# Two layer norms applied behind the projection: the query projection and the first pair of the up projection read the un-normed sum

## The chip, the cores and the metric

The kernel runs on one core of one Trainium2 chip. The metric is the device time of one execution in microseconds (us). A difference of 0.2% (1.8 us) is about what a measurement of this kernel can tell from no change.

## The reference, cut to what matters

Two transformer blocks run one after the other on 256 tokens of width 1024, in fp32. The change lies in the first block, between its token mixer and its feed-forward layer:

```python
def layer_norm(x, g, b):
    mu = xf.mean(-1, keepdims=True)
    var = jnp.square(xf - mu).mean(-1, keepdims=True)
    return (xf - mu) * lax.rsqrt(var + EPS) * g + b

h = hybrid_mixer(x, w_in, ...)                    # ends with ... @ w_out
x = layer_norm(ALPHA * x + h, ln1_g, ln1_b)
h = memory_cross_attention(x, mem, wq, wkv, wo)   # q = x @ wq; softmax attention over 256 memory rows; @ wo
x = layer_norm(ALPHA * x + h, ln2_g, ln2_b)
h = conv_ffn(x, w_up, conv_w, conv_b, w_down)     # u = conv(x @ w_up); (gelu(g) * val) @ w_down
x = layer_norm(ALPHA * x + h, ln3_g, ln3_b)
```

With s the sum before the norm, W a weight matrix and r the reciprocal deviation, `layer_norm(s) @ W = r * ((s * g) @ W - mu * (g @ W)) + b @ W`. The mean and the deviation belong to a token, so they can be applied after the product.

## The kernel before, in words

Activations are kept transposed: `X` holds the residual stream as 8 tiles of 128 features by 256 tokens. A matrix product in fp32 accuracy is made of three products of fp32r operands: each operand is split in a high part (an ACT copy, line 142) and a low part (a DVE subtraction, line 145); `three` (L415) multiplies high by high, low weights by high input, high weights by low input. For the input these parts are `INH` and `INL` (or `HIH` and `HIL`), for the weights `hir` and `lor`.

A **unit** is one product with 256 output features over 8 input tiles (`linears_g`, L435): 48 matmuls of 256 columns, six for each input tile k. Its weights come as two tiles of 4 k each, 512 KB from memory into one of six slots of `raw`; `stage` (L337) splits a tile into one of four buffers of `hir` and `lor`: one ACT copy of 128x1024 and one DVE subtraction of 128x1024. `take` (L381) stages up to three tiles ahead, where a buffer's last reader has already been issued. A tile of the modulation weights of the second block costs one DVE pass instead (`mod_step`, L331, shown as a write to `raw,small`). `linears` of two keys is a **pair**: the two units advance together over k.

Every engine works through its own queue strictly in the order in which this program appends instructions, so an ACT copy of a weight tile that stands behind another ACT instruction waits for it, and the DVE subtraction waits for the ACT copy. All waits are semaphores that the code sets.

The place of the change, in the order of the program:

- Output projection `wout` (L1022): for each of 4 units, `resid` (L853) adds the unit into X on DVE, `stats` (L888) squares it on ACT and sums on DVE. After the third unit ACT loads the table for the square root in advance. `part` (L872) sums over features with one-column matmuls.
- First norm (`layer_norm`, L1017): `finish` (L932) makes mean and reciprocal deviation in small DVE steps and one ACT square root, and spreads them over the partitions with two matmuls (`spread`, L920). `apply` (L963) then normalises X tile by tile on DVE, makes `INH` on ACT and `INL` on DVE.
- Query projection `xq` (L1038): a pair and two units; each unit is copied from PSUM to QC by DVE.
- Cross attention (`xattn`, L1047): a software pipeline of six steps over 4 heads. Of head h, step h makes the logits (PE), maximum, exponential and division (DVE, ACT, DVE); step h+1 the transposes (PE, copied by ACT to PY); step h+2 the product with the values (PE), copied by DVE to OCF and split by `oc.put`.
- `xo` (L1099) is like `wout`, then the second norm (L1105), then the up projection (L1115): the pair `("up", 0)`, `("up", 11)`, then single units `("up", c)`, `("up", 11 + c)`. Each is drained by `conv2` (L519): two ACT passes, then four DVE passes.

## Time and profile before

| | |
|---|---|
| median of 3 runs | 922.05 us (921.49 to 922.28) |
| the profiled execution: time | 921.22 us |
| its span, first to last instruction | 919.4 us |
| mean granted TensorE clock | 0.96 |
| TensorE matmul busy | 859.9 us, 94% |
| VectorE (DVE) busy | 647.6 us, 70% |
| ScalarE (ACT) busy | 486.9 us, 53% |
| DMA | 166.40 MB, mean 181 GB/s |

PE is busy for 94% of the span and its clock is at 2.4 GHz for nearly all of it. Times of single instructions are us from the start of the span. A PE row that stands for several instructions gives the first start and the time to the last end. Busy time is an average over stages; what the change touches lies between about 170 and 300 us.

### The profile page before, as it was taken

What the parts mean: (1) busy time and instruction counts of PE and PEld (TensorE: products, weight loads), DVE (VectorE), ACT (ScalarE), POOL (GpSimd) and SP (SyncE); (2) the same over time, 40 slices, a digit from 0 to 9 for tenths busy, and PEclk for the clock granted to TensorE, in tenths of its full rate; (3) what the DMA queues carried; (4) which work ended last, traced back from release to release, by engine and by line L of the source; (5) the groups of instructions that cost most, each with busy time, mean ns of one, the idle gap of its engine ahead of it and who ended that gap; (6) DMA issues with size and microseconds to landing.
All of it is one profiled execution on the core that took longest, in us unless ns stands there. A gap on an engine that the chain in (4) does not pass through costs nothing.

```text
span 919.4 us, 16216 instructions
## 1 busy us (share of the span) xinstructions
PE 859.9 (94%) x6578; PEld 821.4 (89%) x6578; DVE 647.6 (70%) x986; ACT 486.9 (53%) x680; POOL 6.2 (1%) x15
## 2 busy tenths in 40 slices
PE   5999998989889999999968999999996999999995
PEld 5889986879779999999967999898995999999995
DVE  4775777688678877787766696677877766655443
ACT  5644447444445666654435646788654544444450
POOL 0200000000000000000000000000000000000000
PEclk9999999989999999999977999999997899999998
DMA  9774556846052766569851485564664377765531
GB/s 332 219 234 124 180 180 190 250 155 229 25 161 91 218 185 180 182 189 318 267 182 46 134 264 167 143 187 142 219 192 138 104 240 230 228 208 170 178 111 47
DMA packets 145578, 166.40 MB, mean 181 GB/s; under 512 B 5488, under 2 KB 135536, under 8 KB 145504
## 3 DMA queue, kind: packets, MB, share of 16 engines
q1 hardware_dynamic: 143888, 162.82, 57.0%
q0 software_dynamic: 544, 1.49, 0.7%
q8 instruction: 52, 0.85, 0.4%
q10 hardware_dynamic: 1072, 1.05, 0.3%
q14 instruction: 22, 0.18, 0.1%
HBM read 164.10 MB, written 1.25 MB: 180 GB/s over the span
## 4 chain that ended last, share of the span: by engine, by line
PE 71%; DVE 8%; ACT 4%; issue 1%; DVEq 0%; ACTq 0%
PE ps L166 48%; PE ps L421 22%; DVE X L145 2%; ACT FA L142 2%; DVE lor L145 1%; DVE FA L145 1%; ACT hir L142 1%; ACT L142 1%; DVE FA L149 1%; DVE INL L145 1%; DVE st L145 0%; PE ps L169 0%; ACT SQ L142 0%; DVE X L153 0%; DVE SQ L145 0%
## 5 line engine op out<-in xcount | busy, mean ns | idle before, releaser
L166 PE MATMUL ps<-INH,hir 128*128 128x256 f32 x1320 | 384.4, 291 | 15.9 <-DVE lor L145 10.8
L145 DVE TENSOR_TENSOR lor<-raw,hir 128x1024 fp32r<-128x1024 f32 (+1 forms) x268 | 310.3, 1174 | 123.7 <-ACT hir L142 109.1
L421 PE MATMUL ps<-INL,hir 128*128 128x256 f32 x1320 | 379.4, 287 | 1.2 <-DVE INL L145 0.8
L166 PE MATMUL ps<-INH,lor 128*128 128x256 f32 x1320 | 378.7, 287 | 0.0
L142 ACT ACTIVATE hir<-raw 128x1024 fp32r<-128x1024 f32 (+1 forms) x268 | 266.9, 1015 | 143.4 <-PE ps L421 134.9
L166 PEld LDWEIGHTS ps<-INH,hir 128*128 128x128 f32 x1320 | 258.7, 196 | 23.8 <-issue 11.8
L421 PEld LDWEIGHTS ps<-INL,hir 128*128 128x128 f32 x1320 | 258.4, 196 | 2.8 <-DVE INL L145 2.8
L166 PEld LDWEIGHTS ps<-INH,lor 128*128 128x128 f32 x1320 | 258.8, 196 | 1.1 <-issue 1.0
L166 PE MATMUL ps<-HIH,hir 128*128 128x256 f32 x608 | 173.7, 286 | 0.2 <-DVE lor L145 0.2
L166 PE MATMUL ps<-HIH,lor 128*128 128x256 f32 x608 | 172.0, 283 | 0.0
L421 PE MATMUL ps<-HIL,hir 128*128 128x256 f32 x608 | 172.0, 283 | 0.0
L166 PEld LDWEIGHTS ps<-HIH,hir 128*128 128x128 f32 x608 | 116.6, 192 | 2.1 <-issue 1.2
L166 PEld LDWEIGHTS ps<-HIH,lor 128*128 128x128 f32 x608 | 116.7, 192 | 0.5 <-issue 0.5
L421 PEld LDWEIGHTS ps<-HIL,hir 128*128 128x128 f32 x608 | 116.7, 192 | 0.0
L153 DVE SCALAR_TENSOR_TENSOR FA<-ps,vec,FA 128x254 f32<-128x254 f32 (+2 forms) x130 | 53.2, 473 | 20.9 <-ACT FA L142 20.7
L142 ACT ACT_TABLE_LOAD x43 | 55.2, 1283 | 8.6 <-DVE small L156 5.5
L334 DVE SCALAR_TENSOR_TENSOR raw<-raw,cb 128x1024 f32<-128x1024 f32 x48 | 58.2, 1218 | 0.0
L142 ACT ACTIVATE FA<-ps,vec 128x256 f32<-128x256 f32 x58 | 29.4, 558 | 40.4 <-PE ps L421 40.4
L142 ACT ACTIVATE FA<-ps 128x512 f32<-128x512 f32 x47 | 27.4, 594 | 36.9 <-PE ps L421 30.7
L166 PE MATMUL ps<-FA 128*128 128x256 f32 (+6 forms) x212 | 39.2, 365 | 3.5 <-DVE FA L145 2.7
L142 ACT ACTIVATE HIH<-FA 128x512 fp32r<-128x512 f32 (+2 forms) x34 | 21.3, 628 | 39.3 <-DVE FA L145 17.4
L145 DVE TENSOR_TENSOR HIL<-FA,HIH 128x512 fp32r<-128x512 f32 (+2 forms) x34 | 23.4, 689 | 23.0 <-ACT HIH L142 22.9
(128 smaller groups left out, 634.6 us busy)
## 6 DMA issues: line engine op xcount, KB each, us to landing
raw<-in_w_in SPq DMA_DIRECT2D x64, 512.0 KB, 4.6
raw<-in_mod_wT SPq DMA_DIRECT2D x48, 512.0 KB, 4.5
raw<-in_ffn_w_up SPq DMA_DIRECT2D x44, 512.0 KB, 4.5
...
```

What stands on the lines that cost most here:

```text
L142: return AC.do(lambda e: e.activation(o, i, f, **kw), *w)
L145: return DV.do(lambda e: e.tensor_tensor(o, a, b, op), *w)
L149: return DV.do(lambda e: e.tensor_scalar(o, a, s1, None, op0), *w)
L153: return DV.do(lambda e: e.scalar_tensor_tensor(out=o, in0=a, scalar=s, in1=b, op0=op0, op1=op1), *w)
L166: return PE.do(lambda e: e.matmul(o, l, r, start=start, stop=stop, skip_group_check=True), *w, inc=inc)
L334: return DV.do(lambda e: e.scalar_tensor_tensor(out=w, in0=w, scalar=1.0, in1=CB[:, :], op0=ALU.mult, op1=ALU.mult, accum_out=col), t, t_sc)
L421: return PE.do(lambda e: e.matmul(o, *b, start=False, stop=stop, skip_group_check=True), inc=stop)
```

## The change

- `INH` and `INL` get rows of 260 columns instead of 256. The two columns behind the 256 tokens of each k hold the norm's gamma and beta of that feature.
- In the `wout` phase each unit's new sum in X is at once scaled by gamma into `INH` and `INL` (`norm_in`, `put_scaled`): two more ACT passes and two more DVE passes of 256 per unit. The same is done in the `xo` phase, into the memory of `HIH` and `HIL`.
- All four query units and the first pair of the up projection are made by `late_g`: the same number of matmuls, with 258 columns. Columns 256 and 257 of a result are gamma @ W and beta @ W. Each half of a unit gets a PSUM bank of its own.
- The pair starts directly behind the last unit of `wout` or `xo`. `late_ln` puts the one-column matmuls and the small steps (`moments`) behind the pair's second k, and the matmuls that spread mean and deviation behind its fifth k (`rows_out`); an ACT copy moves them to SBUF.
- A unit is copied out by `normal`: on DVE a 2-column copy and a pass of 256 for each half, and a pass of 512; then two passes of 256 on ACT. Before it was one DVE copy of 512 for `xq`; the units of the up pair are now written to GA and GB and `conv2` reads them there.
- X itself is normalised later: for the first norm by `x_update` (two DVE passes of 512 and two ACT passes of 256), four times: after the second and the third query unit, and after steps 3 and 4 of the cross attention. For the second norm `apply` is kept, since the units from `("up", 1)` on read the normed input; its first three parts are issued behind the pair's fifth k, the fourth after the first `normal`, the fifth after the second.

The diff, cut to its core (`spread` is divided into `diag` and the matmul, `stats` can hand back its last part to be issued later, `apply` becomes a generator `apply_g` that stops after each part):

```diff
+        INHX = sb("INH", 8 * TE, F32R)[:, :].rearrange("p (k t) -> p k t", t=TE)
+        INLX = sb("INL", 8 * TE, F32R)[:, :].rearrange("p (k t) -> p k t", t=TE)
+        INH, INL = INHX[:, :, 0:T], INLX[:, :, 0:T]
...
+        class Late(Inp):
+            def __init__(self, hi, lo, n):
+                super().__init__(hi, lo)
+                self.n, self.ext = n, []
+            def put_scaled(self, k, src, g, *w):
+                a = act(self.hi[:, k, 0:T], src, ACT.Copy, *w, *self.free, scale=g)
+                self.tok[k] = (a, stt(self.lo[:, k, 0:T], src, g, self.hi[:, k, 0:T].bitcast(F32), ALU.mult, ALU.subtract,
+                                      a, *w, *self.free))
+            def vector(self, i, src, *w):
+                h = self.hi[:, :, T + i:T + i + src.shape[2]]
+                a = act(h, src, ACT.Copy, *w, *self.free)
+                b = tt(self.lo[:, :, T + i:T + i + src.shape[2]], src, h.bitcast(F32), ALU.subtract, a, *w, *self.free)
+                self.ext = [a, b]
+        def late_g(keys, x):
+            bs = [(lin.get(), att.get()) for _ in keys]
+            done = [None] * len(keys)
+            PE.wait(*x.ext)
+            for k0 in (0, HALF):
+                ws = [weights(key, k0) for key in keys]
+                for k in range(HALF):
+                    kk = k0 + k
+                    for c, (h, hi, lo, ta, tb) in enumerate(ws):
+                        PE.wait(ta, tb, x.tok[kk][0])
+                        for j, b in enumerate(bs[c]):
+                            if kk == 0:
+                                PE.wait(*b.free)
+                            cs = slice(128 * j, 128 * j + 128)
+                            done[c] = three(b.ap[:, 0:T + x.n], hi[:, k, cs], lo[:, k, cs], x.hi[:, kk, 0:T + x.n],
+                                            x.lo[:, kk, 0:T + x.n], kk == 0, kk == 7, x.tok[kk][1])
+                        if k == HALF - 1:
+                            hfree[h] = [done[c] if kk == 7 else PE.do(PE.todo.pop())]
+                    if kk < 7:
+                        yield
+            return list(zip(bs, done))
...
+        def moments(t):
+            b, n = stb["b"], stb["n"]
+            a = DV.do(lambda e: e.tensor_reduce(SN[:, 0:4], b.ap[:, 0:4 * n].rearrange("p (c i) -> p c i", i=n), AX, ALU.add), t)
+            b.free = [a]
+            a = tt(SN[:, 8:10], SN[:, 0:2], SN[:, 0:2], ALU.mult, a)
+            a = stt(SN[:, 2:4], SN[:, 2:4], LN_EPS, SN[:, 8:10], ALU.add, ALU.subtract, a)
+            a = ts(SN[:, 2:4], SN[:, 2:4], LN_EPS, None, ALU.max, None, a)
+            q = act(SN[:, 4:6], SN[:, 2:4], ACT.Sqrt, a)
+            tm = diag(SN[:, 0:2], 0)
+            recip(SN[:, 6:8], SN[:, 4:6], q)
+            return tm, diag(SN[:, 6:8], 1)
+        MB, RB = st[:, 0, :], st[:, 1, :]
+        def rows_out(ts_):
+            b = att.get()
+            fr = b.free
+            PE.wait(*fr)
+            rows = []
+            for i, row in enumerate((MB, RB)):
+                o = b.ap[:, i * T:(i + 1) * T]
+                t = mm(o, C("ones"), DG[:, i, :, :].rearrange("p m n -> p (m n)"), ts_[i], inc=True)
+                dgf[i] = [t]
+                rows.append(t)
+            t = act(st[:, 0:2, :], wide2(b.ap), ACT.Copy, rows[1])
+            b.free = [t]
+            return tuple((Bank(row), t) for row in (MB, RB))
...
+        def late_ln(g, parts, early=None):
+            n, t, tok, rows = 0, None, None, None
+            while True:
+                try:
+                    next(g)
+                except StopIteration as e:
+                    return e.value, rows
+                n += 1
+                if n == 2:
+                    tok = moments(parts())
+                if n == 5:
+                    rows = rows_out(tok)
+                    if early:
+                        early(rows)
+        def centre(i, unit, n, dst, ts_, *w):
+            bs, t = unit
+            vs = [SMALL[:, 328 + 6 * i + 3 * j:331 + 6 * i + 3 * j] for j in range(2)]
+            for j, b in enumerate(bs):
+                a = copy(vs[j][:, 0:n], b.ap[:, T:T + n], t)
+                a = stt(dst[:, j, :], MB, vs[j][:, 0:1], b.ap[:, 0:T], ALU.mult, ALU.subtract, a, *ts_, *w)
+                b.free = [a]
+            return vs, tt(dst, dst, over(RB, 2), ALU.mult, a)
+        def normal(i, unit, dst, ts_, *w):
+            vs, a = centre(i, unit, 2, dst, ts_, *w)
+            for j in range(2):
+                t = act(dst[:, j, :], dst[:, j, :], ACT.Identity, a, scale=-1.0, bias=vs[j][:, 1:2])
+            return t
...
+        def norm_in(key, kt, inp, xg, gcol, tw, *w):
+            for c in range(4):
+                b, t = linear((key, c), kt, inp)
+                t = resid(c, b, t, *w[c])
+                parts = stats(c, X[:, 2 * c:2 * c + 2, :], t, True, defer=True)
+                for k in (2 * c, 2 * c + 1):
+                    xg.put_scaled(k, X[:, k, :], gcol(k), t, tw)
+            return parts
+        xg = Late(INHX, INLX, 2)
+        xg.free = [PE.now()]
+        xg.vector(0, vec3("ln1_g"), t_vec)
+        xg.vector(1, vec3("ln1_b"), t_vec)
+        parts = norm_in("wout", 8, mix, xg, lambda k: V("ln1_g", k), t_vec, *[[t_x]] * 4)
...
-        two = linears([("xq", 0), ("xq", 1)], 8, x1)
+        two, rows = late_ln(late_g([("xq", 0), ("xq", 1)], xg), parts)
+        t_rows = [rows[0][1], rows[1][1]]
+        t_x1 = []
+        def x_update():
+            c = len(t_x1)
+            xc = X[:, 2 * c:2 * c + 2, :]
+            t = tt(xc, xc, over(MB, 2), ALU.subtract, *t_rows)
+            t = tt(xc, xc, over(RB, 2), ALU.mult, t)
+            t_x1.append([act(X[:, k, :], X[:, k, :], ACT.Identity, t, scale=V("ln1_g", k), bias=V("ln1_b", k))
+                         for k in (2 * c, 2 * c + 1)])
         for c in range(4):
-            b, t = two[c] if c < 2 else linear(("xq", c), 8, x1)
-            tqc.append(copy(QC[:, 2 * c:2 * c + 2, :], wide2(b.ap), t, *ph))
-            b.free = [tqc[-1]]
+            u = two[c] if c < 2 else run(late_g([("xq", c)], xg))[0]
+            tqc.append(normal(c, u, QC[:, 2 * c:2 * c + 2, :], t_rows, *ph))
+            if c in (1, 2):
+                x_update()
...
-        for _ in xattn():
-            pass
-        for c in range(4):
-            b, t = linear(("xo", c), 8, oc)
-            t = resid(c, b, t)
-            t = stats(c, X[:, 2 * c:2 * c + 2, :], t, True)
+        xg = Late(*(v[:, 0:8 * (T + 2)].rearrange("p (k t) -> p k t", t=T + 2) for v in (HIHF, HILF)), 2)
+        xg.free = [PE.now()]
+        for i, _ in enumerate(xattn()):
+            if i in (3, 4):
+                x_update()
+        xg.vector(0, vec3("ln2_g"))
+        xg.vector(1, vec3("ln2_b"))
+        parts = norm_in("xo", 8, oc, xg, lambda k: V("ln2_g", k), t_vec, *t_x1)
...
+        def ln2_start(rows):
+            ln2.append(apply_g(*rows, xs, xs, lambda k: V("ln2_g", k), lambda k: V("ln2_b", k), x2))
+            for _ in range(3):
+                next(ln2[0])
+        two, rows = late_ln(late_g([("up", 0), ("up", 11)], xg), parts, ln2_start)
         hid.free = [PE.now()]
-        two = linears([("up", 0), ("up", 11)], 8, x2)
+        t_rows = [rows[0][1], rows[1][1]]
+        t_up = []
+        for u, dst in zip(two, (GA[1], GB[1])):
+            t_up.append(normal(len(t_up), u, dst, t_rows, *gfree[1]))
+            next(ln2[0], None)
+        for _ in ln2[0]:
+            pass
```

How the instructions stand now. First ACT behind the square root of the first norm. Before (`INH<-X,vec` is the normalised input, `hir<-raw` a weight tile, `FA,small<-ps,small` the exponential of the attention):

```order
L142 ACTIVATE small<-small 128x2
L142 ACTIVATE INH<-X,vec 128x256 x8
L142 ACTIVATE hir<-raw 128x1024 x7
L142 ACT_TABLE_LOAD
L142 ACTIVATE FA,small<-ps,small 128x256 x4
```

And of the change (`FA<-FA,small` are the ACT passes of `normal`, `X<-X,vec` those of `x_update`):

```order
L145 ACTIVATE small<-small 128x2
L145 ACTIVATE hir<-raw 128x1024 x2
L145 ACTIVATE st<-ps 128x512
L145 ACTIVATE FA<-FA,small 128x256 x4
L145 ACTIVATE X<-X,vec 128x256 x2
L145 ACTIVATE hir<-raw 128x1024 x3
L145 ACTIVATE FA<-FA,small 128x256 x2
L145 ACTIVATE X<-X,vec 128x256 x2
L145 ACTIVATE hir<-raw 128x1024 x2
L145 ACTIVATE FA<-FA,small 128x256 x2
L145 ACT_TABLE_LOAD
L145 ACTIVATE FA,small<-ps,small 128x256 x4
```

Seven weight tiles stood together between the last `INH` and the table load of the exponential; now they stand in groups behind passes of `normal` and `x_update`, and the last passes of `normal` stand directly ahead of the table load.

Second, DVE in the query projection of the change, from the end of the second unit's `normal` to the start of the third's (a `normal` is twice `COPY small<-ps` and `FA<-st,small,ps`, then `FA<-FA,st`; `raw,small<-raw,cb` is a modulation tile):

```order
L156 SCALAR_TENSOR_TENSOR FA<-st,small,ps 128x256
L148 TENSOR_TENSOR FA<-FA,st 128x512
L148 TENSOR_TENSOR X<-X,st 128x512 x2
L148 TENSOR_TENSOR lor<-raw,hir 128x1024 x2
L337 SCALAR_TENSOR_TENSOR raw,small<-raw,cb 128x1024
L148 TENSOR_TENSOR lor<-raw,hir 128x1024
L159 COPY small<-ps 128x2
L156 SCALAR_TENSOR_TENSOR FA<-st,small,ps 128x256
```

Before, the same stretch, from the last low part of the input on:

```order
L145 TENSOR_TENSOR INL<-X,INH 128x512
L334 SCALAR_TENSOR_TENSOR raw,small<-raw,cb 128x1024
L145 TENSOR_TENSOR lor<-raw,hir 128x1024 x2
L334 SCALAR_TENSOR_TENSOR raw,small<-raw,cb 128x1024
L156 COPY FA<-ps 128x512 x2
L145 TENSOR_TENSOR lor<-raw,hir 128x1024 x2
L334 SCALAR_TENSOR_TENSOR raw,small<-raw,cb 128x1024
L145 TENSOR_TENSOR lor<-raw,hir 128x1024
L156 COPY FA<-ps 128x512
```

The two weight tiles for the fourth query unit, now rows `lor<-raw,hir 128x1024 x2` behind `X<-X,st 128x512 x2`, stood behind two plain copies.

Third, the end of the cross attention on ACT. Before, from the exponential of the last head:

```order
L142 ACTIVATE FA,small<-ps,small 128x256 x2
L142 ACTIVATE FA<-ps 128x512
L142 ACTIVATE INH<-FA 128x512
L142 ACTIVATE FA<-ps 128x512
L142 ACTIVATE INH<-FA 128x512 x2
```

Of the change:

```order
L145 ACTIVATE FA,small<-ps,small 128x256 x2
L145 ACTIVATE FA<-ps 128x512
L145 ACTIVATE INH<-FA 128x2x256
L145 ACTIVATE X<-X,vec 128x256 x2
L145 ACTIVATE FA<-ps 128x512
L145 ACTIVATE INH<-FA 128x2x256
L145 ACTIVATE X<-X,vec 128x256 x2
L145 ACTIVATE INH<-FA 128x2x256
```

The first `x_update` of this place stands ahead of the copy `FA<-ps` of the last head's transposed probabilities.

Fourth, DVE at the second norm, of the change, from the spread of the deviation to the first convolution:

```order
L148 TENSOR_TENSOR st<-con,small 128x256
L148 TENSOR_TENSOR lor<-raw,hir 128x1024 x2
L148 TENSOR_TENSOR X<-X,st 128x256 x4
L153 TENSOR_SCALAR X<-X,vec 128x256
L148 TENSOR_TENSOR INL<-X,INH 128x256
L148 TENSOR_TENSOR X<-X,st 128x512 x2
L153 TENSOR_SCALAR X<-X,vec 128x256
L148 TENSOR_TENSOR INL<-X,INH 128x256
L159 COPY small<-ps 128x2
L156 SCALAR_TENSOR_TENSOR FA<-st,small,ps 128x256
```

Before, the same stretch began with one `lor<-raw,hir 128x1024` and then `X<-X,ps 128x256 x4`, and no row of `FA` or `small` stood between the parts of the norm. Two `normal` and two weight tiles are now inside it or ahead of it.

## Rows read from the trace of the kernel before

**Rows 1.** The page: busy time by engine, and the chain that ended last.
```profile
PE 859.9 (94%) x6578; PEld 821.4 (89%) x6578; DVE 647.6 (70%) x986; ACT 486.9 (53%) x680; POOL 6.2 (1%) x15
...
PE 71%; DVE 8%; ACT 4%; issue 1%; DVEq 0%; ACTq 0%
```

**Rows 2.** Timeline of PE, both norms: start, duration, line, out<-in, count, idle before.
```profile
192.92 0.28 PE L421 MATMUL ps<-HIL,hir 128*128 128x256 f32 x1
193.04 0.50 PE L166 MATMUL ps<-con,st 128*128 128x1 f32 x4
193.40 0.58 PE L166 MATMUL ps<-con,SQ 128*128 128x1 f32 x4
...
200.61 0.58 PE L166 MATMUL ps<-INH,hir 128*128 128x256 f32 x1 [1.40 <-ACT INH L142]
...
268.23 0.50 PE L166 MATMUL ps<-con,st 128*128 128x1 f32 x4
```

**Rows 3.** Timeline of DVE, first norm.
```profile
191.40 2.36 DVE L145 TENSOR_TENSOR lor<-raw,hir 128x1024 fp32r<-128x1024 f32 x2 [0.57 <-ACT hir L142]
...
196.17 0.17 DVE L940 TENSOR_REDUCE small<-ps 128x4 f32<-128x8 f32 x1 [0.70 <-PE ps L166]
...
197.50 0.42 DVE L145 TENSOR_TENSOR st<-con,small 128x256 f32<-128x256 f32 x1
...
198.98 1.73 DVE L145 TENSOR_TENSOR X<-X,ps 128x256 f32<-128x256 f32 x4
...
209.67 0.69 DVE L145 TENSOR_TENSOR INL<-X,INH 128x512 fp32r<-128x512 f32 x1
```

**Rows 4.** Timeline of ACT, first norm.
```profile
190.25 1.99 ACT L142 ACTIVATE hir<-raw 128x1024 fp32r<-128x1024 f32 x2
...
202.85 1.09 ACT L142 ACTIVATE INH<-X,vec 128x256 fp32r<-128x256 f32 x2 [1.50 <-DVE X L145]
```

**Rows 5.** Windows, first norm: stretch, busy time of each engine, granted clock (PEclk), DMA.
```profile
197.50:200.60 3.10, 1.71 (x4) 0.75 (x4) 2.96 (x6) 0.60 (x1) 0.00 (x0) 0.55 0.16 33
200.60:204.60 4.00, 3.85 (x16) 3.55 (x17) 3.86 (x9) 1.69 (x3) 0.00 (x0) 0.50 0.37 121
```

**Rows 6.** DVE groups by form: count, busy us, mean ns, idle before.
```profile
L153 DVE SCALAR_TENSOR_TENSOR FA<-ps,vec,FA 128x254 f32<-128x254 f32 x58 | 25.0, 471 | 0.0
L145 DVE TENSOR_TENSOR X<-X,ps 128x512 f32<-128x512 f32 x18 | 12.3, 684 | 0.3
...
L145 DVE TENSOR_TENSOR st<-st,X 128x512 f32<-128x512 f32 x3 | 2.1, 684 | 0.0
```

**Rows 7.** PE groups by form.
```profile
L166 PE MATMUL ps<-hir,INL 128*128 128x512 f32 x16 | 6.3, 391 | 0.0
...
L166 PE MATMUL ps<-hir,INL 128*128 128x256 f32 x16 | 4.5, 283 | 0.0
```

**Rows 8.** Timeline of PE, cross attention.
```profile
226.36 3.62 PE L166 MATMUL ps<-FA 128*128 128x256 f32 x16
231.14 0.66 PE L169 MATMUL ps<-con,FA 128*128 128x128 f32 x4 [1.17 <-DVE FA L149]
...
241.75 3.62 PE L166 MATMUL ps<-FA 128*128 128x256 f32 x16
245.01 0.47 PE L166 MATMUL ps<-INH,hir 128*128 128x256 f32 x1
```

**Rows 9.** Timeline of ACT, cross attention.
```profile
224.82 1.28 ACT L142 ACT_TABLE_LOAD   x1
229.22 0.47 ACT L142 ACTIVATE FA<-ps,small 128x256 f32<-128x256 f32 x1 [3.12 <-DVE small L149]
...
242.37 0.58 ACT L142 ACTIVATE FA<-ps 128x512 f32<-128x512 f32 x1
```

**Rows 10.** Timeline of ACT and PE where the up pair and the unit behind it end.
```profile
289.52 1.93 ACT L142 ACTIVATE FA<-ps,vec 128x256 f32<-128x256 f32 x4 [3.69 <-PE ps L421]
...
295.81 0.36 PE L166 MATMUL ps<-INH,hir 128*128 128x256 f32 x1
```

62 lines of the change are left out of this document (33 added, 29 removed).

## Prediction

> **What bounds the kernel now.** I read the page first: PE is busy for 94% of the span and carries 71% of the chain that ended last [rows 1], so DVE and ACT can cost time only where PE waits. The timeline of PE shows such a place at each norm. Behind the last unit of `wout`, at 193.04, PE has only one-column matmuls and the spread until the first query matmul at 200.61 [rows 2]. The reader is to see two losses: the empty time, and the clock. The windows give 0.55 of 2.4 GHz from 197.5 and 0.50, that is 1.2 GHz, from 200.6 to 204.6, back at full behind that [rows 5]. Matmuls of 256 columns follow each other in 0.12 us at full clock (192.92 to 193.04 [rows 2]), a unit of 48 takes 5.76. The cross attention starts on PE at 226.36 [rows 8], so the query pair ended at 226.36 - 96 x 0.12 = 214.84. In the same way the up pair ended 48 x 0.12 and a wait of some 0.08 before the matmul at 295.81 [rows 10], near 289.97. The last `xo` unit ended at 268.23 [rows 2], 75.19 behind 193.04; the second norm repeats the first at that distance.
>
> So much is to be gained: the matmuls of a pair need 11.52 us, and the pairs ended 21.80 and 21.74 behind the last unit, about 10 us lost at each norm.
>
> **Prices.** DVE: a weight or modulation tile 1.13 (pitch in a run: 2.36 for two [rows 3]); a pass of 512 0.68 [rows 6], start to start 0.61; a pass of 256 with PSUM 0.47 [rows 6], start to start 0.36; a copy of 2 columns 0.16, taken from the 8-column reduction on PSUM at 196.17 [rows 3]. One `normal` on DVE: 2 x (0.20 + 0.45) + 0.69 = 1.9, since each pass waits for the one before. An `x_update` on DVE: 1.4. ACT: a weight tile 0.95 to 1.05, a pass of 256 0.60, two 1.09 [rows 4], the table load 1.28 [rows 9].
>
> The norm rows mu and r are now read from SBUF, by DVE. A pass of 512 took 684 ns with PSUM and 684 ns without [rows 6], so I take no gain from this. The Trainium skill, "VectorE: DVE Perf Modes", section "The TRN2 errata — SBUF-src ops pay a fixed extra latency per instruction", gives 62 cycles less for a source in SBUF than in PSUM; by that ten passes of the second norm would be some 0.6 us shorter, an estimate, and the rows speak against it.
>
> 258 columns instead of 256, in 288 matmuls: going from 256 to 512 columns took 391 against 283 ns [rows 7], 0.42 ns a column, so 0.25 us in all. The lower bound is nothing, the upper the whole step to the 512 form, 288 x 0.108 = 31 us. I take 0.25, as 258 is nearest to 256; where PE waits for others it is hidden.
>
> **First norm, walked through the queues** (clock of the trace before). In the `wout` phase each unit gives DVE 0.9 and ACT 1.1 more. Behind the third unit this pushes ACT's two weight tiles (before from 190.25 [rows 4]) by 1.1, and DVE's (before from 191.40 [rows 3]) to end at 194.6. PE doesn't notice, the tiles are ahead. From 193.04 PE runs two k of the pair (2.9), the one-column matmuls (four groups of about 0.36 [rows 2], to 197.4), two k (200.3), the fifth k (201.7). DVE in the meantime: last sum, low parts, a weight tile, a modulation tile, to 200.3; the small steps take 1.75 as before (196.17 to 197.92 [rows 3]), to 202.1. PE waits 0.4, spreads in 0.9 (four matmuls like those of 0.216 below), ends the pair at 207.4: **7.4 us earlier**, and without the empty time in which the clock was lost.
>
> Then the work that was ahead of the pair stands behind it, ahead of weight tiles. DVE: `normal` 206.95 to 208.8, `normal` to 210.75, `x_update` to 212.1. ACT: its `x_update` to 213.1, only then the tile for the fourth query unit, 214.15; DVE's part of it 215.4. PE finished the third unit at 213.2 and waits 2.3; the fourth ends at 221.2. On DVE three more tiles stand ahead of the third `normal` (218.8 to 220.7), then `x_update` 222.0, ACT 223.1 and two tiles 225.1, DVE's 226.5, the fourth `normal` 228.4, ACT's part 229.5. The table for the exponential was loaded at 224.82 in idle time [rows 9]; now it stands behind those passes and ends at 230.8. The first exponential began at 229.22 [rows 9]: **1.6 us later** than before. The gain of 7.4 is gone.
>
> **Cross attention.** From the first exponential on, DVE and ACT set the pace, and PE follows (1.17 waited at 231.14 [rows 8]). The copy of the last head's transposed probabilities, at 242.37 [rows 9], now stands behind an `x_update`: DVE may begin that at 243.1, behind the low part of head 1, ends at 244.5, ACT at 245.5, the copy at 246.1. Its 8 matmuls are the second half of the 16 that began at 241.75, 0.216 apart [rows 8], so they began at 243.5 and will begin at 246.2: **2.7 later**, and `xo` with them (245.01 [rows 8]). The second `x_update` there is hidden by the first `xo` unit.
>
> The clock: PE ends its logits of head 1 at 224.6 and has nothing until 232.7, 8.1 us. Before, this gap was 226.36 + 16 x 0.216 = 229.8 to 231.14, and PE kept its clock. After 193.04 it fell to half at about 197.8, in spite of small matmuls, and came back 4 us into dense work [rows 5]. So I expect 1.2 GHz from about 229 to 237. The logits of head 2 then take 3.4 instead of 1.7, and the chain waits for them: **1.8 later**. First norm and attention together: 1.6 + 2.7 + 1.8 = 6.1 us slower.
>
> **Second norm** (again on the clock of before). The pair runs from 268.23 as above: one-column matmuls behind 271.1, spread at 276.9 to 277.75, end at 282.2, **7.8 earlier**. DVE: deviation 276.0, two weight tiles (freed by the fourth k) to 278.95. Only now the norm begins; its 11.3 us (198.98 to 210.28 [rows 3]) and two `normal` of 1.9 end near 294.0. The next unit, `("up", 1)`, takes input tile 0 at once, tile 1 at 283.6, and then waits: tiles 2 and 3 are split at 288.1, 4 and 5 at 292.7, 6 and 7 at 294.0, so it ends near 295.2, where before it ended at 295.7. Behind that ACT has four convolution passes (1.93 [rows 10]), the Gelu table 1.28, Gelu 0.6 and the tile for `("up", 12)`, to 297.1; DVE's part 298.4. Before, that unit started at 295.81 [rows 10]: **2.75 later**. DVE is then 2.7 behind its old schedule too, so no further wait follows, and none is won back, as PE is full. In these 14 us PE works some 5; if the clock falls, the first 4 us behind 298.4 run at half speed, as they do from 200.6 to 204.6 [rows 5]: 256 columns at 1.2 GHz take 0.213 instead of 0.12, so 4 x (1 - 0.12/0.213) = 1.7 more. I take half of it, 0.9.
>
> **Sum.** 6.1 + 2.75 + 0.9 = 9.8 us slower. The profiled execution took 921.22, 1.8 above its span and 0.8 below the median; 922.05 + 9.8 gives 931.9; I forecast 931.5, as some starts in the walk are rounded late.
>
> **Rivals.**
> Full clock throughout: without both losses the sum is 1.6 + 2.7 + 2.75 = 7.1, 929.1. For it: PE is not empty in the second norm. Against it: rows 5. The Trainium skill, "TensorE: Matmul & The Clock Gate", section "What's actually happening", says that the throttled state is the default and activity releases it, which agrees with rows 5. Chance 0.25.
> Faster: the queues don't hold PE up, only the early start counts, 7.4 + 7.8 = 15.2, 906.9. It decides at one point, the tile for the fourth query unit: if DVE splits it by 213.2 instead of 215.4, and the copy at 242.37 isn't held up, the attention starts early and PE keeps its clock. For it: DVE is busy for 70% only [rows 1], and has no norm to do ahead of the queries. Against it: each queue is in order. Half of it, one place of the two, would be near 915. Chance 0.08.
> Dear columns: a 258-column matmul that costs like 512. 192 stand in the pairs, 192 x 0.108 = 20.7 on top of 9.8, 952. Chance 0.03.
> Cancelled: errors of my walk, or a trace in which `x_update` slips in free time, leave it within 0.2%. Chance 0.04.
> The forecast itself, with the clock lost in at least one place: 0.60.
>
> Slower by over 0.2% (about what a measurement of this kernel can tell from no change): 0.60 + 0.25 + 0.03 = 0.88; the same 0.04; faster 0.08. The range takes in the first two cases, 929 and up to 6.1 + 2.75 + 1.7 = 10.6 or 932.6, and some 3 us of error in each direction for forty chained steps: 926 to 936.
>
> **What would show it.** Right: the query pair ends 14.4 behind the last `wout` unit and the up pair 14.0; PE waits over 2 us for `lor` ahead of the fourth query unit; the first exponential comes directly behind the table load; half the clock in the attention; PE waits for `INL` inside `("up", 1)` and for `lor` behind it. Wrong: a fourth query unit without a wait, an exponential that starts before 229 on the old clock, matmuls of 258 columns more than 0.13 us apart, or the up pair followed by full units.

## The result, and the profile after

The changed kernel took 929.88 us (median of 4 runs, 929.31 to 932.01) against 922.16 (4 runs, 921.49 to 924.05) for the kernel before: a ratio of 1.0085, with a 95% interval of 1.0063 to 1.0106, so 5.8 to 9.8 us slower. The forecast was 931.5, the range 926 to 936. The profiled execution took 929.85, its span is 927.7.

The page of the change: busy time by engine and the chain that ended last, which answer to [rows 1].

```profile
PE 855.3 (92%) x6578; PEld 817.9 (88%) x6578; DVE 656.6 (71%) x1017; ACT 499.2 (54%) x714; POOL 6.2 (1%) x15
...
PE 69%; DVE 9%; ACT 5%; issue 1%; DVEq 0%; ACTq 0%
```

PE is busy for 4.6 us less in a span that is 8.3 us longer, with the same 6578 matmuls. That it is busy for less is a second finding, and it has a section below. The waits of PE from 190 to 320 us say where it stood:

```profile
PE ps L172 <- DVE FA L152: 8.7, 2, 7.7
PE ps L424 <- DVE INL L148: 5.3, 2, 3.6
PE ps L169 <- DVE lor L148: 3.9, 3, 2.3
PE ps L169 <- ACT FA L145: 2.5, 1, 2.5
```

(What it waited for: us in total, times, longest.) Before, the same stretch had:

```profile
PE ps L166 <- DVE st L145: 4.4, 4, 1.3
PE ps L166 <- ACT INH L142: 2.7, 2, 1.4
PE ps L169 <- DVE FA L149: 2.6, 3, 1.2
PE ps L421 <- DVE INL L145: 0.7, 2, 0.3
```

Both waits that the change was to remove, for the sums (`st`) and for the normalised input (`INH`), are gone. Two waits have grown: for the attention's probabilities from 2.6 to 8.7 us, for the low parts of an input (now the input of `("up", 1)`) from 0.7 to 5.3. Two are new: weight tiles, 3.9, and the copy of the last head, 2.5. Timeline of PE of the change, in the columns of [rows 2]:

```profile
195.25 0.28 PE L169 MATMUL ps<-INH,hir 128*128 128x258 f32 x1
196.53 0.36 PE L169 MATMUL ps<-INH,hir 128*128 128x258 f32 x1 [0.39 <-DVE lor L148]
...
218.32 0.36 PE L169 MATMUL ps<-INH,hir 128*128 128x258 f32 x1 [2.32 <-DVE lor L148]
...
235.43 1.12 PE L172 MATMUL ps<-con,FA 128*128 128x128 f32 x4 [7.70 <-DVE FA L152]
236.34 3.62 PE L169 MATMUL ps<-FA 128*128 128x256 f32 x8
...
252.61 1.99 PE L169 MATMUL ps<-FA 128*128 128x256 f32 x8 [2.53 <-ACT FA L145]
254.25 0.47 PE L169 MATMUL ps<-INH,hir 128*128 128x256 f32 x1
...
277.13 0.28 PE L169 MATMUL ps<-HIH,hir 128*128 128x258 f32 x1
...
297.04 0.58 PE L424 MATMUL ps<-INL,hir 128*128 128x256 f32 x1 [3.62 <-DVE INL L148]
301.64 0.58 PE L424 MATMUL ps<-INL,hir 128*128 128x256 f32 x1 [1.67 <-DVE INL L148]
307.67 0.36 PE L169 MATMUL ps<-INH,hir 128*128 128x256 f32 x1 [1.19 <-DVE lor L148]
```

The reader is to see that the pair now starts directly behind the last `wout` unit (195.25) and the last `xo` unit (277.13), and that each wait of the forecast is there: 2.32 ahead of the fourth query unit, 7.70 in the attention with matmuls at half pace behind it (8 in 3.62 where 16 take 3.62 in [rows 8]), 2.53 ahead of the last head's product, two for `INL` and one for `lor`.

**The account.** I count from the end of the last `wout` unit: 193.04 before, 195.25 here. (The 2.2 us between them arose in the first 25 us of the kernel and are told below.)

| us behind the last `wout` unit | before | change | difference |
|---|---|---|---|
| first exponential (229.22; 233.50) | 36.18 | 38.25 | +2.1 |
| `xo` starts (245.01; 254.25) | 51.97 | 59.00 | +7.0 |
| last `xo` unit ends (268.23; 277.13) | 75.19 | 81.88 | +6.7 |
| `("up", 12)` starts (295.81; 307.67) | 102.77 | 112.42 | +9.65 |
| from there to the end of the span | 623.59 | 620.03 | -3.56 |

2.21 + 9.65 - 3.56 is the 8.3 us between the spans. The forecast had +6.1 and +2.75 for the two stages. It had nothing that could give 3.6 us back behind them.

### The profile page after: what moved, and what is told of

Its sections match the earlier page's. It is cut to its first block, busy times and chain, and to the rows that moved or that the text cites. A ratio compares the mean times of both kernels' runs of the same rounds, so it can differ in the third digit from the quotient of the medians.

```text
span 927.7 us, 16289 instructions
## 1 busy us (share of the span) xinstructions
PE 855.3 (92%) x6578; PEld 817.9 (88%) x6578; DVE 656.6 (71%) x1017; ACT 499.2 (54%) x714; POOL 6.2 (1%) x15
## 4 chain that ended last, share of the span: by engine, by line
PE 69%; DVE 9%; ACT 5%; issue 1%; DVEq 0%; ACTq 0%
PE ps L169 47%; PE ps L424 21%; DVE X L148 2%; DVE lor L148 2%; ACT hir L145 1%; ACT FA L145 1%; DVE FA L148 1%; DVE FA L156 1%; ACT INH L145 1%; PE ps L172 1%; ACT L145 1%; ACT X L145 0%; DVE INL L148 0%; ACT SQ L145 0%; DVE FA L152 0%
## 5 line engine op out<-in xcount | busy, mean ns | idle before, releaser
L169 PE MATMUL ps<-INH,hir 128*128 128x256 f32 (+1 forms) x1288 | 374.0, 290 | 19.5 <-DVE lor L148 17.0
L424 PE MATMUL ps<-INL,hir 128*128 128x256 f32 (+1 forms) x1288 | 368.9, 286 | 5.7 <-DVE INL L148 5.5
L169 PE MATMUL ps<-INH,lor 128*128 128x256 f32 (+1 forms) x1288 | 367.3, 285 | 0.0
L424 PEld LDWEIGHTS ps<-INL,hir 128*128 128x128 f32 x1288 | 249.0, 193 | 7.0 <-DVE INL L148 7.0
L169 PEld LDWEIGHTS ps<-INH,lor 128*128 128x128 f32 x1288 | 249.4, 194 | 1.1 <-issue 1.0
L169 PE MATMUL ps<-HIH,hir 128*128 128x256 f32 (+1 forms) x640 | 183.0, 286 | 0.2 <-DVE small L152 0.2
L424 PE MATMUL ps<-HIL,hir 128*128 128x256 f32 (+1 forms) x640 | 181.1, 283 | 0.0
L169 PE MATMUL ps<-HIH,lor 128*128 128x256 f32 (+1 forms) x640 | 181.1, 283 | 0.0
L156 DVE SCALAR_TENSOR_TENSOR FA<-ps,vec,FA 128x255 f32<-128x255 f32 (+2 forms) x122 | 50.0, 472 | 17.5 <-ACT FA L145 17.3
L169 PEld LDWEIGHTS ps<-FA 128*128 128x128 f32 (+2 forms) x212 | 29.9, 181 | 14.2 <-DVE FA L148 3.7
```

The source lines that it names most:

```text
L156: return DV.do(lambda e: e.scalar_tensor_tensor(out=o, in0=a, scalar=s, in1=b, op0=op0, op1=op1), *w)
L169: return PE.do(lambda e: e.matmul(o, l, r, start=start, stop=stop, skip_group_check=True), *w, inc=inc)
L424: return PE.do(lambda e: e.matmul(o, *b, start=False, stop=stop, skip_group_check=True), inc=stop)
```

## The experiments

All twelve ran beside the kernel before, and a ratio is to the runs of that kernel on the same chip. The places are read from each kernel's timeline as in the table above.

| kernel | median, ratio to before (95%) | exponential | `xo` | `("up", 12)` | behind it |
|---|---|---|---|---|---|
| before (first profile) | 922.16 | 36.2 | 52.0 | 102.8 | 623.6 |
| `before_again` | 923.12, one run | 36.7 | 52.5 | 103.2 | 624.8 |
| the change | 929.88, 1.0085 (1.0063 to 1.0106) | 38.25 | 59.0 | 112.4 | 620.0 |
| `first_only` | 927.88, 1.0053 (1.0037 to 1.0068) | 38.25 | 59.5 | 110.3 | 619.1 |
| `second_only` | 922.15, 0.9994 (0.9981 to 1.0007) | 36.4 | 52.2 | 105.6 | 620.7 |
| `tiles_first` | 929.85, 1.0073 (1.0052 to 1.0094) | 39.5 | 60.7 | 114.3 | 619.7 |
| `update_later` | 932.02, 1.0099 (1.0081 to 1.0116) | 38.3 | 55.5 | 112.6 | 620.9 |
| `split_update` | 928.36, 1.0051 (1.0032 to 1.0070) | 35.25 | 53.2 | 113.6 | 619.0 |
| `lean_queries` | 926.48, 1.0038 (1.0019 to 1.0058) | 32.7 | 50.8 | 106.5 | 624.0 |
| `rows_260` | 919.00, 0.9964 (0.9948 to 0.9981) | 36.0 | 51.8 | 102.7 | 619.9 |
| `both_260` | 916.51, 0.9935 (0.9917 to 0.9954) | 36.2 | 52.0 | 102.8 | 617.3 |
| `padded_256` | 915.52, 0.9927 (0.9898 to 0.9956) | 35.8 | 51.6 | 102.4 | 619.2 |
| `distance` | 919.52, 0.9964 (0.9948 to 0.9980) | 36.15 | 51.9 | 102.8 | 620.7 |
| `lean_first` | 917.20, 0.9933 (0.9907 to 0.9959) | 32.9 | 50.9 | 102.5 | 617.8 |

The first two rows are one and the same program, and its two profiles differ by 0.5 us at the exponential and at `xo` and by 1.2 in the last column. So a difference of that size between two single profiles shows nothing.

### Each norm alone

`first_only`: the second norm and the up pair as before.

```diff
-        parts = norm_in("xo", 8, oc, xg, lambda k: V("ln2_g", k), t_vec, *t_x1)
+        for c in range(4):
+            b, t = linear(("xo", c), 8, oc)
+            t = resid(c, b, t, *t_x1[c])
+            t = stats(c, X[:, 2 * c:2 * c + 2, :], t, True)
...
+        layer_norm("ln2_g", "ln2_b", x2, t)
-        two, rows = late_ln(late_g([("up", 0), ("up", 11)], xg), parts, ln2_start)
+        two = linears([("up", 0), ("up", 11)], 8, x2)
```

> The first norm as in the change, the second norm and the up pair as before. My theory (work that stood ahead of the query pair now stands ahead of weight tiles and of the first exponential in the in-order queues of DVE and ACT, and an x_update stands ahead of the last head's copy): slower than before by 6.1 us, by the terms 1.6 + 2.7 + 1.8, so 927 to 930 against 922; the first exponential directly behind the table load, half clock in the attention. Rival, only the early pair counts: faster than before by about 7, near 915. Rival, the larger input rows or the start of the kernel cost something of their own: slower than 930.

`second_only` is the reverse: the `wout` loop, `layer_norm("ln1_g", ...)`, the four copies to QC and the plain attention as before, the rest as in the change.

> The second norm and the up pair as in the change, the first norm, the queries and the attention as before. My theory (the norm's 11 us on DVE now begin only behind two weight tiles, and two normal stand inside it, so the unit behind the pair waits for its input): slower than before by 2.6 to 3.6 us, near 925. Rival, the early pair pays: faster by up to 7.8, near 914. If a cost of another kind lies in the larger input rows, both this kernel and the one with the first norm alone show it, and their two excesses add up to more than the excess of the full change, 7.7 us.

The first norm alone gave 1.0053, 4.9 us slower. The second alone gave no difference, 0.9994, where 2.6 to 3.6 was expected. Yet its trace has both waits for `INL`, and `("up", 12)` starts 2.8 us later than before:

```profile
289.30 0.58 PE L424 MATMUL ps<-INL,hir 128*128 128x256 f32 x1 [3.63 <-DVE INL L148]
293.89 0.38 PE L424 MATMUL ps<-INL,hir 128*128 128x256 f32 x1 [1.67 <-DVE INL L148]
299.92 0.55 PE L169 MATMUL ps<-INH,hir 128*128 128x256 f32 x1 [3.14 <-DVE lor L148]
```

So the mechanism was there, and something else gave 3 us back. The last column of the table shows it in every kernel that is derived from the change: 618 to 621 behind `("up", 12)`, where the code is the old one, against 623.6. (In `lean_queries` other tiles were moved into that stretch.) It also answers the sum of the two halves: 4.9 and -0.6 add up to 4.3 us, not to the 7.7 of the whole change. If each half contains the same gain of some 3 us, counted once too often in the sum, they agree.

### What gave 3 us back: where the input's parts lie in memory

The one thing of the change that reaches those stages is that `INH` and `INL` got 260 columns a row. `rows_260` is the kernel before with that alone:

```diff
-        INH = sb("INH", 2048, F32R)[:, :].rearrange("p (k t) -> p k t", t=T)
-        INL = sb("INL", 2048, F32R)[:, :].rearrange("p (k t) -> p k t", t=T)
+        TE = T + 4
+        INHX = sb("INH", 8 * TE, F32R)[:, :].rearrange("p (k t) -> p k t", t=TE)
+        INLX = sb("INL", 8 * TE, F32R)[:, :].rearrange("p (k t) -> p k t", t=TE)
+        INH, INL = INHX[:, :, 0:T], INLX[:, :, 0:T]
```

> The kernel before, with one edit: INH and INL get rows of 260 columns instead of 256; everything else, instructions and order, stays. In the four profiles with long rows taken so far, 48 matmuls in a row took 5.68 us, in the one with rows of 256 5.76. If the rows' length (or where the tensors behind them then lie) makes the matmul faster, this kernel shows 5.68 too and is faster than before by about 7000 x 0.0017, up to 10 us, and the change hides a gain of that size. If the pace belongs to the chip that the kernel happened to run on, this kernel and the one before have the same pace and the same time within 1.5 us. I expect the second.

The kernel before itself, unchanged, was profiled beside it:

> The kernel before, profiled again, beside the one with rows of 260 columns on the same chip. If the pace of the matmuls belongs to the chip, 48 matmuls take the same in both; if it belongs to the rows, 5.76 here and 5.68 there. The start: the second weight tile came at 15.8 before and at 17.3 to 17.8 in three of the five others; if that is chance, it can be either here.

I had expected no effect, and it has one: 0.9964 (0.9948 to 0.9981), 3.3 us faster than before. Both were profiled on the same chip. A window of full clock in which PE never waits, `before_again` first (stretch, busy time and count of PE, PEld, DVE, ACT, POOL, granted clock, DMA), then `rows_260`:

```profile
330.00:430.00 100.00, 100.00 (x835) 100.00 (x835) 80.84 (x121) 57.10 (x79) 0.00 (x0) 1.00 0.68 209
```

```profile
330.00:430.00 100.00, 100.00 (x845) 100.00 (x845) 80.46 (x121) 57.70 (x80) 0.00 (x0) 1.00 0.68 210
```

835 matmuls in 100 us, then 845 (and 502, then 510, from 740 to 800 us), at the same granted clock and on the same chip. Nothing was changed but the rows of `INH` and `INL` and, with them, where these two and the tensors behind them lie. In the change itself it is 847:

```profile
330.00:430.00 100.00, 100.00 (x847) 100.00 (x846) 82.38 (x127) 59.95 (x84) 0.00 (x0) 1.00 0.63 193
```

Start to start, six such matmuls take 0.720 us in the old place and 0.709 in the new. Some 3100 of them stand behind `("up", 12)`; 3100 x 0.0018 = 5.6 us, of which 3.7 (against the first profile of before) to 4.9 (against the second) arrived.

Is it the length of the rows? `both_260` gives long rows to `HIH` and `HIL` too; `padded_256` keeps rows of 256 and puts 32 unused columns behind `INH` and behind `INL`, so that all tensors begin where they begin in `rows_260`.

```diff
-        INH = sb("INH", 2048, F32R)[:, :].rearrange("p (k t) -> p k t", t=T)
-        INL = sb("INL", 2048, F32R)[:, :].rearrange("p (k t) -> p k t", t=T)
+        INH = sb("INH", 2080, F32R)[:, 0:2048].rearrange("p (k t) -> p k t", t=T)
+        INL = sb("INL", 2080, F32R)[:, 0:2048].rearrange("p (k t) -> p k t", t=T)
```

> The kernel before, with two edits: INH and INL, and also HIH and HIL, get rows of 260 columns of which 256 are used. In the kernel with long rows for INH and INL alone, six matmuls that read these took 0.709 us and six that read HIH and HIL, whose rows stayed at 256, 0.720. Theory (a matmul of 256 columns reads rows of 260 faster than rows of 256): six with HIH and HIL take 0.709 too; the 1920 such matmuls gain up to 1920 x 0.0018 = 3.5 us, of which, as with the first 4176 (7.5 by the pace, 3 in the time), some half arrives: 1 to 3 us faster than with the first alone, 0.4 to 0.7% faster than before, 915.5 to 918. Rival, the pace belongs to the tensor or its place and not to its rows: HIH stays at 0.720 and the time is that of the first kernel, 919.

> The kernel before, with one edit: 32 unused columns behind INH and behind INL, so that all tensors lie where they lie in the kernel with rows of 260, while the rows of INH and INL stay at 256 columns. Theory (the rows decide): six matmuls take 0.720 us everywhere and the time is that of the kernel before within 1.5 us. Rival (where the tensors lie decides): 0.709 and 3 us faster.

The padding alone did as much: `padded_256` has 847 matmuls in the window and took 0.9927 (0.9898 to 0.9956), 6.7 us less than before. Its interval, from four runs, takes in the 0.9935 of `both_260` and overlaps that of `rows_260`; whether it is faster than they are is not shown.

```profile
330.00:430.00 100.00, 100.00 (x847) 100.00 (x846) 80.36 (x121) 57.75 (x80) 0.00 (x0) 1.00 0.68 213
```

So the length of the rows is not needed, and my theory fell. In `padded_256` six matmuls with `HIH` and `HIL` stayed at 0.720, in `both_260` they came down to 0.711, and its time, 916.51, is where it was expected. By then pace and distance went together: the low part lay 8192 or 22528 bytes behind the high part in the slow cases, 8320 or 22880 in the quick ones. The last run took that apart: 32 columns ahead of `INH` (distance kept), 32 behind `HIH` (distance changed).

```diff
+        INH = sb("INH", 2080, F32R)[:, 32:2080].rearrange("p (k t) -> p k t", t=T)
...
+        HIH = sb("HIH", 22 * T + 32, F32R)[:, 0:22 * T].rearrange("p (k t) -> p k t", t=T)
```

> The kernel before, with two edits: 32 unused columns ahead of INH (so INH and INL both begin 128 bytes later and lie 8192 bytes apart as before), and 32 unused columns behind HIH (so HIL lies 22656 bytes behind HIH instead of 22528). So far the pace was quick where the low part lay 8320 bytes behind the high part (with rows of 260 and with rows of 256) and where it lay 22880 behind, and slow at 8192 and at 22528, also where HIH and HIL were shifted together by 256 bytes. Theory (the distance of the low part from the high part decides): six matmuls that read INH or INL take 0.720 us, six that read HIH or HIL 0.706 to 0.711; the time is 1 to 2 us less than before. Rival (what lies where in the memory decides in another way, for example the place of INH alone): INH and INL change their pace, or HIH and HIL do not.

It came out the other way round:

```profile
330.00:430.00 100.00, 100.00 (x844) 100.00 (x843) 80.70 (x123) 57.97 (x81) 0.00 (x0) 1.00 0.66 205
```

`INH` and `INL` became quicker (844; 0.712 us for six) at the old distance, and `HIH` and `HIL` stayed at 0.720 at a new one. The distance alone does not decide either. What is shown is that the place of the operands alone changes the pace by 1 to 2% at an unchanged granted clock, and that this reaches the time; which relation of addresses matters stays open.

### The first norm: is it the order in the queues?

`tiles_first` stages what fits ahead of the first `normal`, with the limits of `take`:

```diff
+        def ahead():
+            n = sum(1 for p in plan[used[0]:staged[0]] if p[3] is not None)
+            while n < AHEAD and staged[0] < len(plan) and (not plan[staged[0]][3] or hfree[nhl[0] % NHL] is not None):
+                n += plan[staged[0]][3] is not None
+                stage()
+        ahead()
         for c in range(4):
```

> The change, with one edit: the weight tile that the fourth query unit waits for is staged ahead of the first normal instead of behind two normal and an x_update. Theory of the queues: PE's wait of 2.3 us ahead of the fourth query unit is gone or below 0.3; the unit ends about 2.3 earlier behind the third; the first exponential comes 1.1 to 2.3 us earlier, counted from the last wout unit; the whole is 1 to 2.3 us faster than the change, 927.6 to 928.9 against 929.9. Rival, DVE's own work sets the exponential (it is as much as before): PE's wait goes, the exponential stays, and the time is that of the change within 0.5.

Neither case came: the time is that of the change, PE still waited (1.81, now ahead of the fourth unit's second half), and the exponential came 1.2 us later. The timeline of DVE shows why:

```profile
210.27 1.23 DVE L148 TENSOR_TENSOR lor<-raw,hir 128x1024 fp32r<-128x1024 f32 x1 [2.32 <-ACT hir L145]
...
215.21 1.41 DVE L148 TENSOR_TENSOR X<-X,st 128x512 f32<-128x512 f32 x2
218.80 1.23 DVE L148 TENSOR_TENSOR lor<-raw,hir 128x1024 fp32r<-128x1024 f32 x1 [2.18 <-ACT hir L145]
```

The tile's buffer is freed only by the pair's last matmul, so ACT starts the copy with the pair's end and DVE stands for 2.32 us ahead of the first `normal`. I had moved a tile and not looked at its buffer. The second wait is the one that counts in the change too: behind an `x_update` DVE stands idle for 2.18 us, because its next tile waits for ACT, whose copy stands behind ACT's half of that same `x_update`, which waits for DVE. It is there twice in the change:

```profile
216.95 2.36 DVE L148 TENSOR_TENSOR lor<-raw,hir 128x1024 fp32r<-128x1024 f32 x2 [2.18 <-ACT hir L145]
...
226.99 2.36 DVE L148 TENSOR_TENSOR lor<-raw,hir 128x1024 fp32r<-128x1024 f32 x2 [2.17 <-ACT hir L145]
```

`split_update` removes it. The DVE half of `x_update` stays, the ACT half is issued a unit or a step later:

```diff
+            owed.append((c, tt(xc, xc, over(RB, 2), ALU.mult, t)))
+        def x_affine():
+            while owed:
+                c, t = owed.pop(0)
+                t_x1.append([act(X[:, k, :], X[:, k, :], ACT.Identity, t, scale=V("ln1_g", k), bias=V("ln1_b", k))
+                             for k in (2 * c, 2 * c + 1)])
...
             u = two[c] if c < 2 else run(late_g([("xq", c)], xg))[0]
+            x_affine()
...
         for i, _ in enumerate(xattn()):
+            x_affine()
             if i in (3, 4):
                 x_update()
+        x_affine()
```

> The change, with one edit: the ACT half of every x_update is issued one unit or one attention step later, behind the weight tiles or behind the copy of the transposed probabilities; its DVE half stays. Theory of the queues: DVE no longer stands still for 2.2 us twice behind an x_update (weight tile, waiting for ACT, waiting for the update), so PE's wait ahead of the fourth query unit falls from 2.3 to 0 to 0.5 us, the first exponential comes 2 to 4 us earlier from the last wout unit (34.3 to 36.3 instead of 38.25, before 36.2), and the copy at the end of the attention no longer waits: xo starts 5 to 7 us earlier than in the change (59.0 to 59.5), near 53. The whole: 4 to 7 us faster than the change, 923 to 926, if the later waits of the change do not grow. Rival: DVE's own work in this stretch, not the order, sets the pace: exponential at 38, time as the change.

The places came nearly as expected. PE's wait is 0.82 instead of 2.32 (0 to 0.5 was expected), and the exponential comes at 35.25, 3.0 earlier than in the change. The copy of the last head no longer waits, and `xo` starts at 53.2, 5.8 earlier. PE still waits 6.16 us for the probabilities, and 8 matmuls behind that take 3.62 us, half the pace:

```profile
215.79 0.36 PE L169 MATMUL ps<-INH,hir 128*128 128x258 f32 x1 [0.82 <-DVE lor L148]
...
231.39 1.11 PE L172 MATMUL ps<-con,FA 128*128 128x128 f32 x4 [6.16 <-DVE FA L152]
232.30 3.62 PE L169 MATMUL ps<-FA 128*128 128x256 f32 x8
```

So the order in the queues is shown to be the cause there. The time followed only in part, by 1.5 us in the medians (928.36 against 929.85 to 929.88) and 3.1 by the ratios, where 4 to 7 was expected. The gain was lost at the second norm. DVE was not ready for the earlier `xo`: its first weight tiles there start 6.3 us behind the first `xo` matmul, in the change 3.8. The up pair waited for a weight tile (1.77 at 273.24), and the clock fell. Windows of `split_update`:

```profile
270.60:273.20 2.60, 0.86 (x8) 0.66 (x6) 2.07 (x4) 2.11 (x3) 0.00 (x0) 1.00 0.22 76
273.20:277.00 3.80, 3.76 (x24) 3.79 (x24) 3.33 (x6) 2.14 (x4) 0.00 (x0) 0.71 0.73 194
277.00:281.00 4.00, 4.00 (x20) 4.00 (x20) 2.60 (x8) 0.44 (x2) 0.00 (x0) 0.50 0.53 160
281.00:285.00 4.00, 4.00 (x20) 4.00 (x20) 0.47 (x2) 1.18 (x2) 0.00 (x0) 0.50 0.15 53
```

The granted clock is 0.50 for 8 us in which PE is full, 20 matmuls in 4 us instead of 34.

`update_later` tests the term of 2.7 alone, by moving the two updates of the attention behind it:

```diff
-        for i, _ in enumerate(xattn()):
-            if i in (3, 4):
-                x_update()
+        for _ in xattn():
+            pass
+        x_update()
+        x_update()
```

> The change, with one edit: the two x_update of the cross attention (after its steps 3 and 4) are issued behind its last step, ahead of the input vectors of the second norm. Theory: the copy of the last head's transposed probabilities no longer waits behind an x_update, xo begins 2.7 us earlier counted from the first exponential, and nothing waits for the two updates later, since the first xo unit takes 5.8 us: 927.2 against 929.9. Rival, the step is given back because the two updates then delay the weight tiles or the sum behind the first xo unit: PE shows a new wait inside xo and the gain is below 1 us.

The term is real: from the first exponential to the start of `xo` it is 17.2 us, against 20.75 in the change (59.00 - 38.25). The rival is true as well: the up pair waits 2.96 for a tile, `("up", 12)` starts where it did, and the kernel gained nothing: its median, 932.02, is the highest of all, with an interval that overlaps that of the change. The place of this wait, in `split_update` and in `update_later`:

```profile
273.24 0.35 PE L169 MATMUL ps<-HIH,hir 128*128 128x258 f32 x1 [1.77 <-DVE lor L148]
```

```profile
279.20 0.36 PE L169 MATMUL ps<-HIH,hir 128*128 128x258 f32 x1 [2.96 <-DVE lor L148]
```

Of the 3.5 us some 0.7 is not the term's: it arises between the first and the last exponential, 12.4 us here and 13.1 in the change, ahead of the updates that were moved. I put it down to the clock, which came back earlier in this profile; `first_only`, with the updates in their old place, has 12.4 too.

`lean_queries` is `split_update` with two edits more, which take work off DVE and ACT in this stretch: three modulation tiles to the down projection, and the exponential's table loaded ahead of the last `normal`.

```diff
-        add2(("xq", 0), A["xa_wq"], 0, ("xq", 1), A["xa_wq"], 256, mod=1)
+        add2(("xq", 0), A["xa_wq"], 0, ("xq", 1), A["xa_wq"], 256)
...
-            add(("down", c), A["ffn_w_down"], 256 * c, 22, mod=3, spread=True)
+            add(("down", c), A["ffn_w_down"], 256 * c, 22, mod=3 + int(c < 3), spread=True)
...
+            if c == 3:
+                preload(ACT.Exp)
```

> As the one with the split update, and two edits more: the three modulation tiles of the query phase are moved to the down projection of this block, where DVE has time, and ACT loads the exponential's table in advance, ahead of the last normal. Theory: DVE is relieved of 3 x 1.13 us ahead of the exponential and ACT of 1.28 directly ahead of it; the exponential comes 30 to 33 us behind the last wout unit, against 36.2 in the kernel before, and xo starts near 47 to 50, against 52.0: 3 to 6 us faster than the kernel with the split alone, 919 to 922. Rival: PE or another wait sets the exponential: the same as the split alone.

The exponential came at 32.7, 3.5 us ahead of the kernel before, as expected; `xo` came only 1.2 ahead, at 50.8 and not at 47 to 50. The kernel took 926.5, not 919 to 922, since `("up", 12)` still starts 3.7 us late by the second norm. `lean_first` therefore combines this first norm with the old second norm (the edit of `first_only`) and rows of 260 everywhere (`both_260`).

> The first norm as in the change with its queues relieved (the ACT half of x_update issued later, the three modulation tiles of the query phase moved to the down projection, the exponential's table loaded in advance), the second norm and the up pair as before, and rows of 260 everywhere. In the kernel with both norms this first part ended the xo phase 73.9 us behind the last wout unit, against 74.7 in the kernel with long rows alone. Theory: freed of the queues the early query pair is worth about 1 us: 0 to 1.5 us faster than the kernel with long rows everywhere of the same job. Rival: the later tiles or the four x_update cost it again in the xo phase, 1 to 3 us slower than that kernel; then the early pair does not pay in any of the orders tried.

917.20 against 916.51 for `both_260` on the same chip, ratios 0.9933 and 0.9935: no difference. `("up", 12)` starts at 102.5 and 102.8. With the queues relieved so far, the early query pair is worth 0.3 us by the trace, which is less than two profiles of one kernel differ by, and nothing that the time can show. Its exponential came 3.3 us earlier than in `both_260`. The attention then gave 2.3 of that back between its first and last exponential (13.2 us against 10.9), where the clock fell. PE of `lean_first`, timeline and windows:

```profile
229.57 1.11 PE L171 MATMUL ps<-con,FA 128*128 128x128 f32 x4 [3.58 <-DVE FA L151]
230.48 3.62 PE L168 MATMUL ps<-FA 128*128 128x256 f32 x8
```

```profile
227.00:231.00 4.00, 1.43 (x6) 1.34 (x7) 2.12 (x7) 2.32 (x9) 0.00 (x0) 0.72 0.38 117
231.00:236.00 5.00, 5.00 (x16) 4.06 (x15) 1.64 (x5) 1.80 (x8) 0.00 (x0) 0.54 0.00 0
```

A PE that arrives early at a chain that DVE and ACT pace waits longer there, 3.58 us instead of 1.17 in [rows 8], and runs behind the wait at a granted clock of 0.54, which is 1.2 GHz for most of that window.

## Why the prediction was right, and what it owes to luck

**The places were right.** The query pair was to end 14.4 us behind the last `wout` unit. DVE waits for its end and starts to copy it out 14.3 behind (209.56 - 195.25):

```profile
209.56 0.16 DVE L159 COPY small<-ps 128x2 f32<-128x2 f32 x1 [1.10 <-PE ps L424]
```

The up pair was to end 14.0 behind the last `xo` unit, and the next unit starts directly behind it at 291.26, 14.1 behind 277.13. The wait ahead of the fourth query unit was forecast at 2.3 and is 2.32. The first exponential comes directly behind the table load:

```profile
231.28 0.91 ACT L145 ACTIVATE FA<-FA,small 128x256 f32<-128x256 f32 x2 [3.45 <-DVE FA L148]
232.21 1.28 ACT L145 ACT_TABLE_LOAD   x1
233.50 0.47 ACT L145 ACTIVATE FA<-ps,small 128x256 f32<-128x256 f32 x1
```

**The terms.** Exponential later: 1.6 forecast, 2.07 measured; a wait of 0.39 for a tile in the pair was not in the walk. The clock in the attention: 1.8 forecast. The last exponential is read out 51.34 us behind the last `wout` unit against 47.11, so 4.23 - 2.07 = 2.16. No run takes the clock alone away; but `second_only` and `rows_260`, which keep it, need 10.9 us from the first to the last exponential, as before, and every kernel with the early query pair 12.1 to 13.2. The `x_update` ahead of the last copy: 2.7 forecast, 7.03 - 4.23 = 2.80 measured, and this is the order that causes it (ACT of the change):

```profile
250.99 1.09 ACT L145 ACTIVATE X<-X,vec 128x256 f32<-128x256 f32 x2 [2.09 <-DVE X L148]
251.98 0.57 ACT L145 ACTIVATE FA<-ps 128x512 f32<-128x512 f32 x1
```

Together 7.03 for 6.1. The second norm: 2.75 forecast; from the last `xo` unit to `("up", 12)` 30.54 against 27.58, 2.96. The expected 1.2 GHz in the attention is there, 0.50 from 231 to 240 us, and came back inside the next window:

```profile
231.00:235.40 4.40, 0.00 (x0) 0.00 (x0) 1.83 (x7) 3.21 (x7) 0.00 (x0) 0.50 0.45 123
235.40:240.00 4.60, 4.57 (x14) 3.75 (x15) 1.52 (x6) 1.51 (x5) 0.00 (x0) 0.50 0.00 0
240.00:244.00 4.00, 4.00 (x19) 3.58 (x18) 2.33 (x6) 1.93 (x6) 0.00 (x0) 0.85 0.00 0
```

**The term that did not come** is the 0.9 for the clock behind the second norm. I had halved it, being unsure. In the change the clock fell inside the waits for `INL`, where slow matmuls only shortened the wait for `lor`, and was back ahead of `("up", 12)` (1.00 from 306.2 to 311):

```profile
301.60:306.20 4.60, 4.56 (x21) 4.57 (x22) 4.48 (x11) 4.57 (x8) 0.00 (x0) 0.51 0.00 0
```

In `second_only` it fell one wait later and covered full work, 19 matmuls in 4.1 us. There the term is paid at the place; behind `("up", 12)` as a whole that kernel took 620.7, against 620.0 in the change and 619.1 in `first_only`, so at most 1.5 us of it can be seen:

```profile
299.90:304.00 4.10, 4.08 (x19) 4.10 (x20) 4.10 (x7) 2.67 (x5) 0.00 (x0) 0.50 0.66 187
```

**What the sum lacked.** "258 columns instead of 256" asked only what the two columns cost, and found 0.25 us. The size holds: six matmuls of 258 columns take 0.720 us, in `INH` and in `HIH`, and six of 256 in the new place 0.709 with `INH` and 0.720 with `HIH`, so in the 192 that read `INH` it is some 0.35 us. But the term did not ask what new addresses do to every other matmul that reads `INH`. That is worth -3.3 us, by `rows_260`. Against that placement the mechanism costs 1.0085 / 0.9964 = 1.0121, 11.2 us, with the two intervals combined some 8.7 to 13.7; by the two profiles, from the last `wout` unit to the end, it is 732.45 - 722.63 = 9.8. The halves agree: 1.0053 / 0.9964 gives 8.2 us for the first norm (forecast 6.1; by the profiles 7.0) and 0.9994 / 0.9964 gives 2.8 for the second (forecast 2.75, and 0.9 for the clock). So the sum of 9.8 holds within what can be measured, with its first norm 1 to 2 us too small and its clock term 0.9 too large.

**Luck.** That the forecast came out only 1.6 us high is in part luck. Between the two profiles, the stages that it walked through cost 9.65 us (its terms without the last: 8.85, and 9.75 with it). Two things of which it knew nothing stand beside them: 3.56 us less behind `("up", 12)`, and 2.21 us more in the first 25 us of the kernel, which `distance`, with the old code for all stages, has as well. Without that late start the change would have looked some 6 us slower, not 8. How often the late start came in the runs that were not profiled is not known.

**Taking nothing for the source of mean and deviation** was right: `X<-X,st` of 512 columns, read from SBUF, took 688 ns in 14 instances, `X<-X,ps`, from PSUM, 683. The rule of the Trainium skill, "VectorE: DVE Perf Modes", section "The TRN2 errata — SBUF-src ops pay a fixed extra latency per instruction", that a source in SBUF is quicker by 62 cycles, is not borne out by this pair of rows.

**The rivals.** "Faster" made the wait ahead of the fourth unit and the last copy its test. With both nearly gone in `split_update` `xo` starts 5.8 us earlier than in the change, and still 1.2 later than before: PE waits for the probabilities all the same and loses its clock there, and then once more at the second norm. The rival overlooked that an early PE only waits at the next chain. "Dear columns" and "full clock" are refuted by the rows above.
